# A hybrid decoder block on one core: the projections in Strassen form

## The reference

```python
h = rms_norm(z, norm_w[l])
p = (h @ w_in[l] + b_in[l])                       # 1024 -> 8 x 1024
q, fz, iv, g_hg, u, g_pool, m_hg, m_pool = split(p)
# mixer 1: gated linear recurrence (8 heads of 128), chunk by chunk, gate f = lb + (1-lb)*sigmoid(fz), k = 1 - f
o = hgrn2_chunkwise(q, k, iv, log_f)
y_hg = (rms_norm(o, hg_norm_w) * silu(g_hg)) @ w_down_hg
# mixer 2: trailing-window means (2, 4, 8, 16) minus the token, one 256-wide matrix per group
y_pool = (mixed * pool_scale * silu(g_pool)) @ w_down_pool
merged = sigmoid(m_hg) * y_hg + sigmoid(m_pool) * y_pool
out = rms_norm(z + merged @ w_out, final_norm_w)[:, 16:]
```

## Time and profile before

| | |
|---|---|
| median of 3 runs | 1176.2 us (1176.16 to 1176.2) |
| the profiled execution | 1176.21 us, span 1174.7 us |
| TensorE busy, weight loads busy | 1157.8 us, 1017.0 us |
| VectorE, ScalarE, GpSimd busy | 584.3, 314.3, 77.9 us |
| granted TensorE clock, mean over the span | 0.997 of full speed |
| moved by DMA | 78.16 MB |

### The profile page before, as it was taken

How to read it: one execution, slowest core, us unless ns; L and a number is a source line. 1 busy time by engine, 2 the same in 40 slices (tenths; PEclk the granted TensorE clock), 3 DMA queues, 4 the chain that set the end, 5 groups by cost and what they waited for, 6 DMA issues and landing times. The chain is left out here.

```text
span 1174.7 us, 17070 instructions
## 1 busy us (share of the span) xinstructions
PE 1157.8 (99%) x6700; PEld 1017.0 (87%) x6700; DVE 584.3 (50%) x948; ACT 314.3 (27%) x550; POOL 77.9 (7%) x135
## 2 busy tenths in 40 slices
PE   8999999999999999999999999999999999999996
PEld 8998989898998989888888888889889898888885
DVE  6474847575665757464401111114465576657233
ACT  7422223122313222222212222222333323222222
POOL 2200000000000000000000000000000000112111
PEclk9999999999999999999999999999999999999998
DMA  6111100011111011112122122122111110446123
GB/s 224 50 37 36 37 27 29 34 36 36 36 36 34 19 36 36 36 63 73 63 99 81 54 80 80 61 73 72 45 60 39 45 53 30 166 144 225 61 99 117
DMA packets 22288, 78.16 MB, mean 67 GB/s; under 512 B 3280, under 2 KB 3280, under 8 KB 22256
## 3 DMA queue, kind: packets, MB, share of 16 engines
q1 hardware_dynamic: 15008, 54.60, 13.7%
q0 software_dynamic: 6960, 22.59, 5.8%
q10 hardware_dynamic: 288, 0.53, 0.1%
HBM read 65.13 MB, written 12.58 MB: 66 GB/s over the span
## 5 line engine op out<-in xcount | busy, mean ns | idle before, releaser
L769 PE MATMUL acc<-h_hi,w_hi 128*128 128x512 f32 (+3 forms) x1232 | 445.0, 361 | 0.7 <-DVE h_lo L1031 0.7
L769 PE MATMUL acc<-h_hi,w_lo 128*128 128x512 f32 (+3 forms) x1232 | 436.6, 354 | 0.0
L769 PE MATMUL acc<-h_lo,w_hi 128*128 128x512 f32 (+3 forms) x1232 | 436.2, 354 | 0.0
L769 PEld LDWEIGHTS acc<-h_hi,w_hi 128*128 128x128 f32 x1232 | 231.9, 188 | 26.0 <-DVE h_lo L1031 0.9
L769 PEld LDWEIGHTS acc<-h_hi,w_lo 128*128 128x128 f32 x1232 | 231.6, 188 | 25.2
L769 PEld LDWEIGHTS acc<-h_lo,w_hi 128*128 128x128 f32 x1232 | 231.9, 188 | 23.7
L1042 DVE TENSOR_TENSOR w_lo<-raw,w_hi 128x1024 fp32r<-128x1024 f32 x80 | 97.8, 1223 | 168.7 <-ACT w_hi L473 168.7
L769 PE MATMUL acc<-a_hi,w_lo 128*128 128x512 f32 x256 | 99.7, 389 | 0.0
L769 PE MATMUL acc<-a_hi,w_hi 128*128 128x512 f32 x256 | 99.7, 389 | 0.0
L769 PE MATMUL acc<-a_lo,w_hi 128*128 128x512 f32 x256 | 99.6, 389 | 0.0
L473 ACT ACTIVATE w_hi<-raw 128x1024 fp32r<-128x1024 f32 x80 | 84.2, 1052 | 14.9 <-DMA part_spill<-part 3.8
(11 more groups left out here) (179 smaller groups left out, 1404.0 us busy)
## 6 DMA issues: line engine op xcount, KB each, us to landing
raw<-in_wstream SPq DMA_DIRECT2D x88, 512.0 KB, 3.4
xin<-in_x SPq DMA_DIRECT2D x8, 512.0 KB, 4.0
smp_spill<-gm POOLq DMA_DIRECT2D x16, 256.0 KB, 2.3
part_spill<-part POOLq DMA_DIRECT2D x16, 256.0 KB, 2.3
sp_in<-smp_spill POOLq DMA_DIRECT2D x16, 256.0 KB, 3.0
pt_in<-part_spill POOLq DMA_DIRECT2D x16, 256.0 KB, 3.7
xr<-in_x POOLq DMA_DIRECT2D x16, 256.0 KB, 3.3
out_z<-row SPq DMA_DIRECT2D x8, 512.0 KB, 3.8
```

The source lines that it names most:

```text
L769: ins = pe.matmul(out_ap, a, b, start=first and n == 0, stop=final and n == 2)
```

## The change

The 80 projection blocks (all but `out`) become 40 pairs of blocks. A pair is a 256 x 1024 matrix times 1024 x 1024 (the tokens without meta): the weights in 2 x 2 parts of 128 x 512, the input in 2 x 2 parts of 512 channels x 512 tokens. In the Strassen-Winograd form seven products of a 128 x 512 weight part and a 512 x 512 input part replace eight. A product is 12 matmuls of 512 columns (4 k-blocks, three passes). Four of the seven weight operands that aren't plain are sums S1 to S4, made by VectorE for each pair (`weight_sums`); the seven input operands (`R_B11` ... `R_V4`) are made once at the start (`first_low`, `second_sums`, `v_high`, `v_low`) and lie split in SBUF, 7 x 16 KB a partition, in the place of h. The products of a pair are added up in `acc` banks and on the way out: product 0's bank is copied by ScalarE (`copy_first`) before product 2 is added onto it, and so on; VectorE adds the quarters 11, 22 and 12 (`add_11`, `add_22`, `add_12`), ScalarE takes the last (`last_quarter`). The weights' halves go through a ring of four, three products ahead (`high`, `low`; `ahead` on VectorE).

The meta tokens of the F, V and U blocks are no part of this: in the products 0, 1, 3 and 6 of the 12 pairs FV and U, `meta_product` adds 8 matmuls of 32 and 16 columns.

Since the input operands fill SBUF, the gated output a, the pool result c and the gates MH and MP go to HBM (`store_a`, `store_spill` and the like on GpSimd's queue). Ahead of the down_hg and the down_pool pairs (DH, DP) a or c is loaded again (4 MB), and the seven operands are made from it (`stage_sum`, ScalarE's `operand_high`, `operand_low`, called by `rebuild` on VectorE). The order of the stages is: heads with pairs (F, V) and (Q, G); MP; pool groups; MH; DH; DP; out. All loops are written out. The gates' scalings and the copies of `prepare` move from VectorE to ScalarE, and the bias is added in the copies.

The core of the diff, added lines (and, in VectorE's head, kept ones); removed are the counterparts described above (`half_unit`, the `Fori` head bodies, `split_hi`, `split_lo`).

```diff
+def pair_table():
+    pairs = []
+    for j in range(HEADS):
+        pairs.append(("FV", (F, j), (V, j)))
+        pairs.append(("QG", (Q, j), (G, j - 1)) if j else ("QM", (Q, 0), (MP, 0)))
+    pairs += [("MM", (MP, 1), (MP, 2)), ("MG", (MP, 3), (G, HEADS - 1))]
+    pairs += [("MM", (MP, 4), (MP, 5)), ("MM", (MP, 6), (MP, 7))]
+    for g in range(4):
+        pairs += [("U", (U, 2 * g), (U, 2 * g + 1)), ("PG", (PG, 2 * g), (PG, 2 * g + 1))]
+    pairs += [("MH", (MH, 2 * i), (MH, 2 * i + 1)) for i in range(4)]
+    pairs += [("DH", ("down_hg", 2 * i), ("down_hg", 2 * i + 1)) for i in range(4)]
+    pairs += [("DP", ("down_pool", 2 * i), ("down_pool", 2 * i + 1)) for i in range(4)]
+    return pairs
...
+ORDER = [(0, 0), (0, 1), (1, 0), (1, 1)] + [(0, i) for i in range(2, 7)] + [(1, i) for i in range(2, 7)]
+ORDER += [(p, i) for p in range(2, N_PAIRS) for i in range(PRODUCTS)]
...
+QUARTERS = ((0, 0), (1, 1), (0, 1), (1, 0))
...
+        r_hi = [at(f"r_hi{n}", [P, KH, HALF], F32R, R_AT + n * 16384) for n in range(7)]
+        r_lo = [at(f"r_lo{n}", [P, KH, HALF], F32R, R_AT + n * 16384 + 8192) for n in range(7)]
...
+        def bank_of(p, i):
+            return acc[p % 2] if i in (0, 2, 4, 6) else acc[2] if i == 1 else acc[3]
...
+            def store_a(r):
+                for t in range(2):
+                    pool.wait_ge(S["a_made"], 2 * r + t + 1)
+                    after(pool, a_stored[t], 16 * r)
+                    pool.dma_start(a_dram[r, t], gt[:, t * HALF:(t + 1) * HALF]).then_inc(a_stored[t], 16)
...
+            def high(o):
+                p, i = ORDER[o]
+                if i in SUM_OF:
+                    act.wait_ge(S["sums_made"], 4 * p + SUM_MADE[SUM_OF[i]])
+                else:
+                    n = 1 if i == 6 else 0
+                    act.wait_ge(raw_loaded[(2 * p + n) % RAWS], raw_count(p, n))
+                after(act, S["mm_done"], o - RING + 1)
+                act.activation(w_hi[o % RING][:, :], operand(o), ACT.Copy).then_inc(S["w_hi"], 1)
...
+            def copy_first(p):
+                act.wait_ge(S["mm_done"], POS[p, 0] + 1)
+                if p:
+                    act.wait_ge(S["added"], ADDED[p - 1, 11])
+                leave(first[:, :], bank_of(p, 0)[:, :], bias_of(p, 0)).then_inc(S["copied"], 1)
...
+            def during(p, i):
+                if i == 0:
+                    extra(p - 1, 2)
+                    last_quarter(p - 1)
+                    if p - 1 in META_AT:
+                        meta_half(p - 1, 1)
+                elif i == 1:
+                    copy_first(p)
+                elif i == 2 and p in META_AT:
+                    meta_half(p, 0)
+                elif i == 3:
+                    copy_second(p)
+                    extra(p, 0)
+                elif i == 4:
+                    copy_fifth(p)
+                elif i == 6:
+                    extra(p, 1)
+                if POS[p, i] + 3 < N_PROD:
+                    high(POS[p, i] + 3)
...
+                for k in range(KH):
+                    w = slice(k * P, (k + 1) * P)
+                    pe.matmul(bank[:, 0:2 * META], w_hi[slot][:, w], hm[:, c, k, :], start=i in (0, 3) and k == 0,
+                              stop=False)
+                    ins = pe.matmul(bank[:, 0:META], w_lo[slot][:, w], hm[:, c, k, 0:META], start=False,
+                                    stop=i in (1, 6) and k == KH - 1)
...
+            def half(p, i, part):
+                slot, bank = POS[p, i] % RING, bank_of(p, i)
+                    if i == 0:
+                        after(pe, S["c21_done"], p - 1)
+                    elif i == 1:
+                        bank_b_free(p)
+                    elif i == 2:
+                        pe.wait_ge(S["copied"], COPIED[p, 1])
+                    elif i == 3:
+                        if p:
+                            pe.wait_ge(S["added"], ADDED[p - 1, 12])
+                        if p in META_AT:
+                            pe.wait_ge(S["meta_added"], META_AT[p] + 1)
+                    elif i == 4:
+                        pe.wait_ge(S["copied"], COPIED[p, 2])
+                    elif i == 5:
+                        pe.wait_ge(S["copied"], COPIED[p, 5])
+                    else:
+                        pe.wait_ge(S["added"], ADDED[p, 22])
+                    operands_ready(p, i)
+                elif p in META_AT and i in (0, 1, 3, 6):
+                    meta_product(p, i)
+                for k in (2 * part, 2 * part + 1):
+                    ins = three(bank[:, :], (w_hi[slot][:, w], w_lo[slot][:, w]), (r_hi[i][:, k, :], r_lo[i][:, k, :]),
+                                i in (0, 1, 3) and k == 0, k == KH - 1, True)
...
+            for j in range(1, HEADS + 1):
+                r = j - 1
+                for n in range(2 * PRODUCTS):
+                    p, i = fv(j) + n // PRODUCTS, n % PRODUCTS
+                    if n == 2:
+                        step(r, 1)
+                    elif n == 8:
+                        step(r, 3)
+                    elif n == 9:
+                        step(r, 4)
+                    elif n == 10:
+                        step(r, 5)
+                    elif n == 11:
+                        k_transposes(r)
+                    elif n == 12:
+                        k_times_v(r)
+                    elif n == 13:
+                        outputs(r)
+                    half(p, i, 0)
+                    if n == 0:
+                        step(r, 0)
+                    elif n == 1 and r:
+                        o_transposes(r - 1)
+                    elif n == 4:
+                        v_transposes(r)
+                    elif n == 5:
+                        step(r, 2)
+                    half(p, i, 1)
...
+            def second_sums(i):
+                dve.wait_ge(S["h_hi"], i)
+                c = slice((i - 5) * P, (i - 4) * P)
+                upper = banks_of(i)[1]
+                k = 4 * (i - 5)
+                dve.tensor_tensor(r_lo_f[R_V5][:, :, c], b11_whole[:, :, c], r_lo_f[R_B22][:, :, c], ALU.subtract) \
+                    .then_inc(S["v_made"], 1)
+                dve.tensor_tensor(r_lo_f[R_V7][:, :, c], upper, r_lo_f[R_B22][:, :, c], ALU.subtract) \
+                    .then_inc(S["v_made"], 1)
+                dve.wait_ge(S["v_made"], k + 1)
+                dve.scalar_tensor_tensor(r_lo_f[R_V6][:, :, c], upper, -1.0, r_lo_f[R_V5][:, :, c], ALU.mult,
+                                         ALU.subtract).then_inc(S["v_made"], 1)
+                dve.wait_ge(S["v_made"], k + 3)
+                dve.scalar_tensor_tensor(r_lo_f[R_V4][:, :, c], r_lo_f[R_V6][:, :, c], -1.0, r_lo_f[R_V4][:, :, c],
+                                         ALU.mult, ALU.subtract).then_inc(S["v_made"], 1)
+                dve.tensor_tensor(r_lo[R_B22][:, :, c], upper, r_hi[R_B22][:, :, c].bitcast(F32), ALU.subtract) \
+                    .then_inc(S["h_lo"], 1)
...
+            def weight_sums(p):
+                for n in range(2):
+                    dve.wait_ge(raw_loaded[(2 * p + n) % RAWS], raw_count(p, n))
+                a11, a12, a21, a22 = raw_half(p, 0, 0), raw_half(p, 0, 1), raw_half(p, 1, 0), raw_half(p, 1, 1)
+                done = S["sums_made"]
+                dve.tensor_tensor(sums[S1][:, :], a21, a22, ALU.add).then_inc(done, 1)
+                dve.tensor_tensor(sums[S3][:, :], a11, a21, ALU.add).then_inc(done, 1)
+                dve.wait_ge(done, 4 * p + 1)
+                dve.tensor_tensor(sums[S2][:, :], sums[S1][:, :], a11, ALU.add).then_inc(done, 1)
+                dve.wait_ge(done, 4 * p + 3)
+                dve.tensor_tensor(sums[S4][:, :], sums[S2][:, :], a12, ALU.add).then_inc(done, 1)
...
+            def add_22(p):
+                quarter_free(p, 1)
+                dve.wait_ge(S["mm_done"], POS[p, 4] + 1)
+                dve.wait_ge(S["copied"], COPIED[p, 5])
+                dve.scalar_tensor_tensor(quarter(p, 1, 1), bank_of(p, 4)[:, :], -1.0, fifth[:, :], ALU.mult,
...
+            second_sums(5)
+            x_mean(7)
+            h_row(7)
+            low(3)
+            v_low(5)
+            second_sums(6)
+            x_mean(8)
+            h_row(8)
+            add_11(0)
+            weight_sums(0)
+            v_low(6)
+            second_sums(7)
+            low(4)
+            meta_add(0, 0)
+            v_low(7)
+            second_sums(8)
+            low(5)
+            add_11(1)
+            v_low(8)
+            low(6)
+            low(7)
+            dve.wait_ge(S["lb_exp"], 1)
...
+                p, q, r = fv(j), qg(j), j - 1
+                has_meta = p in META_AT
+                ahead(p, 0)
+                if r:
+                    mean_o(r - 1)
+                ahead(p, 1)
                 level(r, 0)
+                if r:
+                    normalise_o(r - 1)
+                add_11(p)
+                if r:
+                    gate(r - 1, 0)
+                ahead(p, 2)
+                if r:
```

(136 more changed lines are left out.)

1745 lines of the change are left out of this document (969 added, 776 removed).

## The result

The changed kernel takes 1275.8 us (median of 4 runs, 1273.2 to 1276.0) against 1176.2 (4 runs as well): 1.0842 times as long, interval 1.0823 to 1.086. It is slower, as forecast, but 48 us slower than the forecast's 1228 and outside its range. The profiled execution has a span of 1274.0 us.

What follows compares the result with a forecast made beforehand. The kernel was taken as a TensorE queue, time being matmul starts times pitch. 1174.7 - 118 + 48 + 41 + 28.5 + 20 + 22.5 + 10 = 1226.7, with 1.5 above the span 1228 us, 4.4% slower; range 1170 to 1262, the forecast's own 1195 to 1258.

Steps and rivals of the forecast that it cites:

- Clock after the new waits: Some ten waits over 5 us may halve the clock, each return costing up to 2.5 us: +10, bounds 0 and 25.
- the 2.5 us in the start: Start: after TensorE's 14 us standstill, slow clock as in the earlier trace's first small matmuls adds 2.5 us.
- if the granted clock falls for long: Sign that the prediction is wrong, named beside the o-transposes finding their input ready.
- TensorE's work, -118 and +48: Projections: fewer matmul starts, 882 to 764 us, -118; 384 small meta matmuls at 0.112 plus shape changes, +48.
- 48 changes of shape: Meta products on TensorE: 48 switches of matmul shape at 0.1 us each, counted within the +48.
- Rival 2: The 384 small meta matmuls go at their columns' pace, 0.027 us each: 1193 us; chance 0.08.
- Heads, +41: Walk through a head: TensorE waits 5.2 us for VectorE's normalised o, 6.1 in all in heads 2 to 7: +41.
- Start, +28.5: Product 0 at about 26 us, product 2 of pair 0 at 62 behind VectorE's 36 us: 52.5 against 24.
- Pool, +20: Product 6 of the PG pairs waits for `add_22` behind window sums: waits of 8.7, 6.2, 3.6 and 1.1.
- Rebuild and end, +22.5: Rebuilding operands from a and c: waits 6.5 and 8, c load 3, end 3, last head's o-transposes 2.
- Rival 1: TensorE stays fed: waits behind VectorE's order in heads, pool and rebuild don't appear: 1142 us; chance 0.14.
- Rival 3: VectorE bounds the head, 72 us instead of 66.7, and the clock stays low in gaps: +37 + 15, 1280; chance 0.08.

Runs made afterwards that it cites:

- h1_filled: Changed kernel plus 18 unread 512-column matmuls in TensorE's wait before the o-transposes, heads 2 to 8: 1251.6 us, 1.0641 times the kernel before.
- f_all2: `o_all` with unread 128-column matmuls in eleven TensorE waits, half as many as `f_all`, and the first meta half's addition earlier: 1193.2 us, 1.0148.
- o_start: `h3_order` with other instruction orders in the start on TensorE, VectorE and ScalarE, nothing added or left out: 1219.5 us, 1.0376.
- c_early: Changed kernel with the 4 MB of c loaded two quarters earlier in the down projection: 1265.6 us, 1.077 times the kernel before.
- h3_order: Changed kernel with the two o-normalising instructions moved in VectorE's queue to directly behind the mean: 1227.4 us, 1.0438 times the kernel before.
- o_all: `h3_order` with both sets of other orders, those of `o_start` and `o_late`, nothing added or left out: 1198.6 us, 1.0186.
- f_all: `o_all` with unread 128-column matmuls before eleven TensorE waits, and the first meta half's addition earlier: 1210.6 us, 1.0287.
- h2_half_filled: Changed kernel plus 9 unread 512-column matmuls in TensorE's wait before the o-transposes, heads 2 to 8: 1267.6 us, 1.0769 times the kernel before.
- o_late: `h3_order` with other orders behind the heads (pool, rebuilds, c load, last head's o), nothing added or left out: 1202.8 us, 1.0218.

## Why the prediction was wrong

**The step that failed is "Clock after the new waits", +10, with the 2.5 us in the start.** 12.5 us were forecast, 57.8 measured; that is 45 of the 48 us. Both factors were too small. The number of waits was taken as ten, those over 5 us (six heads, though the forecast's own walk has this wait in seven); waits of 2.0 and 2.9 us were followed by slow phases as well, and 22 waits of TensorE are longer than 2 us. And the price taken was 1 us a wait, between the bounds of 0 and 2.5; over the 22 waits it is 2.6 us each. The 2.5 came from the only slow phase in the trace before that has matmuls in it, 6.24 us of small matmuls at the start; in the heads it is 3.5 us a wait, because 4 to 9 us of work lie in the phase. The bounds 0 to 25 were no bounds: nothing in the earlier trace rows limits the number of waits, and the upper price was a guess from one case. The forecast did name this as a sign of being wrong, "if the granted clock falls for long", and it is the sign that came. `h1_filled` is the proof by removal for the heads: order untouched, clock held, 24.2 us gone (between the two profiles 24.9, of them 21.2 in the heads) and the head at 66.1. Behind the heads `f_all2` shows the same on a smaller scale. For the start it is shown by executions of the same code (last section).

The Trainium skill, "Perfetto Trace Analysis", section "Matmul Optimizations", says that matmuls should run back-to-back in batches, since the engine scales its power with utilisation. `h1_filled` agrees, with 24.2 us for work that nobody reads; the forecast cited this rule and gave it 10 us.

**TensorE's work, -118 and +48: right, the 48 by 5 too high.** The small matmuls start 0.111 apart (0.112 said). The 0.1 for each of 48 changes of shape stood in no row, and it is not there: in a U pair a product with its eight small matmuls takes 3.62 us (693.71 to 697.33 on TensorE's timeline) and twelve of 512 columns take 2.72, so 0.90 for eight and 43 in all. With 43 the sum of three parts is 4 us, 0.3%, short of the span, and up to 0.8% in the runs above; what fills that is open. Rival 2, the pace of columns, is out.

**Heads, +41: the path right, 3 us less.** 4.89 us instead of 5.2 in the heads 2 to 8, by the walk's own path; all waits of the heads together are 38 us more than before. With the clock held a head takes 66.1, for the forecast 66.7 (its own terms add up to 67.0).

**Start, +28.5: the waits right in sum, the walk not.** Product 0 came at 25.6 (26 said), product 2 of pair 0 at 68.2 instead of 62. The waits of the start are 25 us more than before, with one of 3.48 at 100.3, for the 26 that are left of the term without its 2.5 of clock; the 6 us by which product 2 is late are clock loss (9.8 us up to there), and so are part of the 45 above. The walk has VectorE at work from 26 us on without a stop. VectorE had less to do there than said (32.4 us, not 36), but stood still for 7.6 us in one piece. Tile 5's transposes stand behind product 0 in TensorE's queue, and product 0 ran at half clock:

```profile
32.56 1.91 PE L1098 MATMUL levels<-ident,hrow 128*128 128x128 f32 x8
35.62 0.69 DVE L1305 TENSOR_TENSOR r_lo_f<-b_whole,r_lo_f 128x512 f32<-128x512 f32 x1 [7.56 <-ACT r_hi L651]
```

The forecast has one hole on TensorE, of 14 us; there are two, of 7.4 and 11.5. `o_start` takes the transposes out from behind the product, and then VectorE's work does set the time, at 60.1.

**Pool, +20:** 1.10, 2.89, 5.43 and 7.50 for 1.1, 3.6, 6.2 and 8.7, 3 us less than said.

**Rebuild and end, +22.5: 32.** 4.83 and 6.67 for 6.5 and 8; 3.02, 2.86 and 2.03 near the end for 3; 2.93 for 2 in pair 18; 1.04 more. The mis-sized one is the c load: 8.80 for 3. The forecast counted its transfer against VectorE's sums and left out what it is queued ahead of, the gates of the next quarter (14.0 us from issue to landing for the slowest, 4.4 for the median one); `c_early` moves it and saves 7.9 us behind the heads.

**The rivals.** Rival 1 (no waits) did not occur: its waits are all there. Rival 3 came nearest in time (1280), and that is luck: it has the low clock in it, but at less than half of the 57.8 us, and its 37 us of a VectorE-bound head are not there; `h3_order` has a head of 62.3 us. VectorE's order, not its load, makes the heads' waits.

**What the seven-product form is worth here.** Its matmuls are worth 70 to 75 us, and none of the eleven versions run had less than 77.9 us of waits and fillers together (`o_all`). The best, 1193.2, is 1.5% slower than the kernel before. Most of what is left is the start's hole of 14 us and waits of 1 to 5 us where VectorE makes operands. Whether an order exists that wins was not settled.

## What to carry to other kernels

When a change turns a dense TensorE queue into one with waits, price each wait twice: its length, and the work behind it at half clock (here, by the windows, 3.5 us for a wait of 4.9, 2.3 for one of 2.9), and count the waits of 2 to 3 us too. Ask of each engine's written order which instruction the busiest engine waits for, and what stands ahead of it that it does not need; two instructions moved were worth 48 us, and a wait that can't be moved is cheaper when filled, as long as the filler ends before the wait does (`f_all` overran and lost 12 us) and another engine does not set the time. For a large transfer, ask what is queued behind it, not only whether it arrives in time.

## What had not been expected of the hardware

Waits of about 2.9 us have no fixed price. In `h2_half_filled` seven equal waits of 2.86 us were followed at once by half clock, by half clock some us later, or by full clock, and the runs of one changed kernel spread by 1.6 to 7.8 us, where the kernel before repeats within 0.3 us.

The start shows where some of that spread comes from. Six of the profiled kernels have the same start. In two profiles (the changed kernel and `h2_half_filled`) the clock was at half from 18 to 35 us, 17 us in one piece; in four (`h1_filled`, `h3_order`, `c_early`, `o_late`) it was so for 3.4 us only, at 17 or at 25 us. Product 2 of pair 0 began at 68.1 and 68.2 in the first group, with 9.8 us of clock loss ahead of it, and at 63.9 to 65.1 in the second, with 4.0 to 4.4. So a gain of a few us read from one profile each is not the edit's unless the stretch that was edited shows it.

A matmul of 128 columns on f32 operands shows two records of 0.11 us, so 0.22 us in all, as much as one of 512 columns on fp32r.
